# Two piece buffers in the accumulator for the first part, and another order of the projection pieces, in a two-layer hybrid mixer kernel

## The reference, cut to what matters

```python
def hybrid_layer(x, ...):
    h = rmsnorm(x, pre_norm)
    proj = einsum('bld,de->ble', h, w_in)          # columns of all three mixers and their gates
    o_a = rmsnorm(gated_deltanet(silu(conv(q,k,v)), ...)) * silu(gz)   # 4 heads of 128, chunk recurrence
    o_b = rmsnorm(ssd(silu(conv(x,B,C)), ...) * silu(sz))              # 2 groups of 8 heads
    o_c = rmsnorm(retention(rotary(q), rotary(k), v)) * silu(rg)       # 4 heads of 128
    out = einsum('ble,ed->bld', concat(o_a, o_b, o_c), w_out)
    return x + rmsnorm(out, post_norm)
```

## Time and profile before

| | us |
|---|---|
| median of 3 runs | 2120.73 (2119.14 to 2121.55) |
| the profiled execution | 2119.12 |
| its span, first to last instruction | 2117.3 |
| PE (matmul) busy | 2044.3 (97%) |
| PE weight loads busy | 1880.9 (89%) |
| DVE busy | 1416.7 (67%) |
| ACT busy | 878.2 (41%) |
| POOL busy | 482.3 (23%) |

### The profile page before, as it was taken

How to read it: one execution, slowest core, us unless ns; L and a number is a source line. 1 busy time by engine, 2 the same in 40 slices (tenths; PEclk the granted TensorE clock), 3 DMA queues, 4 the chain that set the end, 5 groups by cost and what they waited for, 6 DMA issues and landing times. The chain is left out here.

```text
span 2117.3 us, 38295 instructions
## 1 busy us (share of the span) xinstructions
PE 2044.3 (97%) x14628; PEld 1880.9 (89%) x14628; DVE 1416.7 (67%) x3428; ACT 878.2 (41%) x1771; POOL 482.3 (23%) x432
## 2 busy tenths in 40 slices
PE   7989999999999999999999999999999999999997
PEld 6768889999889998899888888889989899989997
DVE  5788866745578787623668887875466878575334
ACT  5544367423433236511444433754324433563011
POOL 3433343432000012100333333423300001120001
PEclk9989999999999999999999999999999999999999
DMA  6754546668544365454575554857656354573434
GB/s 244 247 179 152 204 173 210 239 212 305 189 170 161 138 207 189 163 166 146 185 262 198 199 194 154 299 191 252 239 206 214 133 170 139 178 270 130 159 106 184
DMA packets 98198, 410.59 MB, mean 194 GB/s; under 512 B 11169, under 2 KB 12257, under 8 KB 84193
## 3 DMA queue, kind: packets, MB, share of 16 engines
q1 hardware_dynamic: 97440, 407.73, 55.1%
q10 hardware_dynamic: 576, 0.41, 0.1%
HBM read 256.93 MB, written 151.16 MB: 193 GB/s over the span
## 5 line engine op out<-in xcount | busy, mean ns | idle before, releaser
L1327 PE MATMUL ps<-w_hi,hT_hi 128*128 128x256 f32 x1792 | 524.3, 293 | 6.7 <-POOL w_low L2389 5.0
L1327 PE MATMUL ps<-w_hi,hT_lo 128*128 128x256 f32 x1792 | 503.4, 281 | 0.0
L1327 PE MATMUL ps<-w_low,hT_hi 128*128 128x256 f32 x1792 | 501.9, 280 | 0.0
L2389 POOL TENSOR_TENSOR w_low<-w_loaded,w_hi 128x512 fp32r<-128x512 f32 x208 | 283.5, 1381 | 429.0 <-ACT w_hi L2103 429.0
L1327 PEld LDWEIGHTS ps<-w_hi,hT_hi 128*128 128x128 f32 x1792 | 337.7, 188 | 13.7 <-POOL w_low L2389 6.3
L1327 PEld LDWEIGHTS ps<-w_low,hT_hi 128*128 128x128 f32 x1792 | 338.1, 189 | 4.4 <-issue 3.8
L1327 PEld LDWEIGHTS ps<-w_hi,hT_lo 128*128 128x128 f32 x1792 | 339.5, 189 | 0.0
L1327 PE MATMUL ps<-hT_hi,w_hi 128*128 128x512 f32 x768 | 319.5, 416 | 6.3 <-POOL w_low L2389 6.2
L1327 PE MATMUL ps<-hT_lo,w_hi 128*128 128x512 f32 x768 | 304.0, 396 | 0.0
L1327 PE MATMUL ps<-hT_hi,w_low 128*128 128x512 f32 x768 | 303.4, 395 | 0.0
L1327 PE MATMUL ps<-wo_parts,mixT_hi 128*128 128x256 f32 x960 | 270.0, 281 | 0.0
(11 more groups left out here) (215 smaller groups left out, 3792.6 us busy)
## 6 DMA issues: line engine op xcount, KB each, us to landing
w_loaded<-in_w_in SPq DMA_DIRECT2D x104, 512.0 KB, 5.0
w_split<-w_hi SPq DMA_DIRECT2D x52, 1024.0 KB, 8.2
w_split<-w_low SPq DMA_DIRECT2D x52, 1024.0 KB, 10.2
w_hi<-w_split SPq DMA_DIRECT2D x104, 512.0 KB, 6.3
w_low<-w_split SPq DMA_DIRECT2D x104, 512.0 KB, 7.1
wo_loaded<-in_w_out SPq DMA_DIRECT2D x32, 512.0 KB, 4.2
wk<-cum_rows SPq DMA_DIRECT2D x32, 512.0 KB, 5.0
wo_split<-wo_parts SPq DMA_DIRECT2D x32, 512.0 KB, 8.5
```

The lines of the kernel that those rows point to most:

```text
L1327: return nc.tensor.matmul(o, a, b, start=start, stop=stop)
L2389: tt(w_lo[at], wr[at], w_hi[at], ALU.subtract)\
```

## The change

It does four things. It swaps pieces in `PIECES`, so that gate pieces stand between the deltanet heads' pieces (the same 26 pieces, in all four parts). In part 0 it gives deltanet heads 2 and 3 buffers of their own in `acc` (`SPARE` = 2, `slot_at`), and so moves on who has to be through before a buffer is used again (`slot_owner`). It writes the rule for split and kept pieces as functions with an exception list `AGAIN`, which is empty. And it changes numbers of the planner. No arithmetic of the kernel changes. The diff, cut: left out are the other places where `slot[:, n % SLOTS, ...]` becomes `slot_at(n)[:, ...]`, and the planner's and engines' uses of `is_split` and `is_kept`, which replace `p % 2 == 0`.

```diff
-PIECES = ([("gz", 0), ("gdn", 0), ("gdn", 1), ("gz", 1), ("bc", 0), ("gdn", 2), ("gdn", 3), ("bc", 1),
-           ("gdn", 4), ("sz", 0, 0), ("gdn", 5), ("sx", 0, 0), ("sx", 0, 1), ("sz", 0, 1), ("sx", 1, 0), ("sz", 1, 0),
+PIECES = ([("gz", 0), ("gdn", 0), ("gdn", 1), ("gz", 1), ("bc", 0), ("gdn", 2), ("bc", 1), ("gdn", 3),
+           ("sz", 0, 0), ("gdn", 4), ("sz", 0, 1), ("gdn", 5), ("sz", 1, 0), ("sx", 0, 0), ("sx", 0, 1), ("sx", 1, 0),
            ("sx", 1, 1), ("sz", 1, 1)]
           + [("ret", i) for i in range(N_RET)])
+AGAIN = range(0)
 SLOTS = 2
+SPARE = 2
...
             elif part == "sum":
-                mark("n", dve(900, *after))
+                mark("n", dve(1200, *after))
...
             elif part == "column":
-                mark("n", dve(len(cols) * 2 * (150 + 2 * BASE), *after))
+                mark("n", dve(len(cols) * 2 * (220 + 2 * BASE), *after))
...
-OUT_WAIT = 2500
+OUT_WAIT = 4000
-KEEP = 8
+KEEP = 2
-HOLD = 0
+HOLD = 250
-SLICE, LINE, TURN, UNIT, TABLE, MB, LANDING = 705, 224, 109, 24 * 119, 1283, 3500, 2300
+SLICE, LINE, TURN, UNIT, TABLE, MB, LANDING = 705, 224, 109, 24 * 119, 1283, 3300, 2000
...
+def is_split(n):
+    p, i = divmod(n, len(PIECES))
+    return p % 2 == 0 or i in AGAIN
+def is_kept(n):
+    p, i = divmod(n, len(PIECES))
+    return p % 2 == 0 and i not in AGAIN
...
+def slot_owner(n):
+    if n is None or n < SLOTS + SPARE:
+        return None
+    return n - SLOTS - SPARE if n < 2 * SLOTS + SPARE else n - SLOTS
...
 def frees(p, i, half):
     need = []
     n = slot_of(p, i, half)
-    if n is not None and n >= SLOTS:
-        need.append(slot_reader(n - SLOTS))
+    if slot_owner(n) is not None:
+        need.append(slot_reader(slot_owner(n)))
...
+        def slot_at(n):
+            if SLOTS <= n < SLOTS + SPARE:
+                return acc[:, 2 * (n - SLOTS):2 * (n - SLOTS) + 2, :].rearrange("p t d -> p (t d)")
+            return slot[:, n % SLOTS, :]
...
-                        sp.wait_ge(w_kept[n % W_RING], kept_done(n - W_RING))
+                        if kept_done(n - W_RING):
+                            sp.wait_ge(w_kept[n % W_RING], kept_done(n - W_RING))
```

More of the change, by code:

```diff
@@ L215, in front_steps @@
                     j, odd = divmod(Q * half + q - SPLIT_FROM, 2)
-                    if 0 <= j < 4 and not odd and (p + (i == len(PIECES) - 1)) % 2 == 0 and (p, i) != (PARTS - 1, len(PIECES) - 1):
+                    if 0 <= j < 4 and not odd and len(PIECES) * p + i + 1 < PARTS * len(PIECES) and is_split(len(PIECES) * p + i + 1):
                         add(("split", *((p, i + 1) if i + 1 < len(PIECES) else (p + 1, 0)), j))
@@ L264, in load_piece @@
         for half in range(2):
-            at["w_in", n, half] = dma(MB if n // len(PIECES) % 2 else MB // 2, *after)
+            at["w_in", n, half] = dma(MB // 2 if is_split(n) else MB, *after)
     def loaded_after():
@@ L278, in needs @@
             kk = q if wide else 2 * q % KD
-            out = [("w_in", n, kk // 4) if p % 2 else ("w_lo", n, kk // 2)] if half == 0 else []
+            out = [("w_lo", n, kk // 2) if is_split(n) else ("w_in", n, kk // 4)] if half == 0 else []
             if q == 0:
@@ L418, in play @@
                 load_piece(n + W_RING, ("n", ))
-            elif p % 2 == 0:
+            elif is_kept(n):
                 dma(2 * MB, ("w_lo", n, 3))
@@ L805, in unit_split_no @@
     return u - GROUPS * UNITS * ((u // (GROUPS * UNITS) + 1) // 2)
+def is_split(n):
[4 more added lines that the diff above has]
+    return p % 2 == 0 and i not in AGAIN
 def split_no(n):
-    return n - len(PIECES) * ((n // len(PIECES) + 1) // 2)
+    return sum(is_split(m) for m in range(n))
 def loads_done(n):
-    return sum(32 if m // len(PIECES) % 2 else 16 for m in range(n % W_RING, n + 1, W_RING))
+    return sum(16 if is_split(m) else 32 for m in range(n % W_RING, n + 1, W_RING))
 def kept_done(n):
-    return sum(32 for m in range(n % W_RING, n + 1, W_RING) if m // len(PIECES) % 2 == 0)
+    return sum(32 for m in range(n % W_RING, n + 1, W_RING) if is_kept(m))
 def slot_of(p, i, half):
@@ L1086, in mtile @@
                 n = slot_of(p, i, half)
-                return 24 * p + NTH[m], m, slot[:, n % SLOTS, (m % 3) * HALF:(m % 3 + 1) * HALF]
+                return 24 * p + NTH[m], m, slot_at(n)[:, (m % 3) * HALF:(m % 3 + 1) * HALF]
             if kind == "bc":
@@ L1093, in mtile @@
                 n = slot_of(p, i, half)
-                return 24 * p + NTH[16 + 4 * g + j], 16 + 4 * g + j, slot[:, n % SLOTS, j * HALF:(j + 1) * HALF]
+                return 24 * p + NTH[16 + 4 * g + j], 16 + 4 * g + j, slot_at(n)[:, j * HALF:(j + 1) * HALF]
             return None
@@ L1120, in hybrid_kernel @@
             loads.append((where[release] if n >= W_RING else -5 if n == 0 else -2, n, ("in", p, i)))
-            if p % 2 == 0:
+            if is_kept(n):
                 loads.append((where["proj", p, i, 0, Q - 1], n, ("keep", p, i)))
@@ L1156, in slot_wait @@
         def slot_wait(eng, n):
-            if n is None or n < SLOTS:
+            if slot_owner(n) is None:
                 return
-            r = slot_reader(n - SLOTS)
+            r = slot_reader(slot_owner(n))
             if r[0] == "gdn_open":
@@ L1383, in _ @@
                         if half == 0 and kk % 2 == 0 and (wide or v == 0):
-                            if p % 2 == 0:
+                            if is_split(n):
                                 pe.wait_ge(S["w_lo_ready"], 4 * split_no(n) + kk // 2 + 1)
@@ L1441, in _ @@
                         for c in range(NT):
-                            i = turn(b[:, c * P:(c + 1) * P], slot[:, n % SLOTS, j * HALF + c * P:j * HALF + (c + 1) * P])
+                            i = turn(b[:, c * P:(c + 1) * P], slot_at(n)[:, j * HALF + c * P:j * HALF + (c + 1) * P])
                         close(i, tag)
@@ L1445, in _ @@
                     h = s[2]
-                    own = slot[:, (10 * p + h) % SLOTS, :]
+                    own = slot_at(10 * p + h)[:, :]
                     b = opened(s)
@@ L1562, in _ @@
                         for j in range(4):
-                            i = turn(b[:, j * P:(j + 1) * P], slot[:, n % SLOTS, j * HALF + c * P:j * HALF + (c + 1) * P])
+                            i = turn(b[:, j * P:(j + 1) * P], slot_at(n)[:, j * HALF + c * P:j * HALF + (c + 1) * P])
                         close(i, tag)
@@ L1609, in _ @@
                     oo = ("ret_oo", p, h)
-                    vv = slot[:, (10 * p + 6 + h) % SLOTS, 1024:1536].rearrange("p (t n) -> p t n", t=NT)
+                    vv = slot_at(10 * p + 6 + h)[:, 1024:1536].rearrange("p (t n) -> p t n", t=NT)
                     if c == 0:
@@ L1734, in _ @@
                             dve.wait_ge(S["ret_sum"], m)
-                        own = slot[:, (10 * p + 6 + h) % SLOTS, half * 512:half * 512 + 512]
+                        own = slot_at(10 * p + 6 + h)[:, half * 512:half * 512 + 512]
                         b = bank(tag).rearrange("p (t q e n) -> p t q e n", t=2, q=2, e=2)
-                        ns = slot[:, (10 * p + 6 + h) % SLOTS, 0:1024].rearrange("p (t q e n) -> p t q e n", t=NT, q=2, e=2)
+                        ns = slot_at(10 * p + 6 + h)[:, 0:1024].rearrange("p (t q e n) -> p t q e n", t=NT, q=2, e=2)
                         r0 = own.rearrange("p (t q e n) -> p t q e n", t=2, q=2, e=2)
```

8 lines of the change are left out of this document (4 added, 4 removed).

## The result

The changed kernel takes 2142.39 us in the median of 4 runs (2136.62 to 2144.84), the kernel before 2119.93 beside it: a ratio of 1.0099, 95% interval 1.0087 to 1.0111. It is 22.5 us slower. I had forecast 2105.

The account below looks back on a forecast made before the run. PE was taken as the bound nearly everywhere, with gains only from its idle time and half clock. 8 + 4 + 3 = 15 us off 2119.1 gave 2104, forecast as a 2105 median (chance 0.52, range 2097 to 2114).

Parts of the forecast that it names:

- Step 4: Planner's new numbers, outside part 0: PE steps placed where they can run; -3 us, bounds -8 and +10.
- Step 1: Part 0: the wait at gdn 4 goes, the gap moves to sz 1 0; gain 8 us, bounds -3 and +14.
- t: Part 0: time of deltanet head 1's mix_turn, 220.22 us before; taken as 217, between 211 and 228.
- the late one: Part 0, late end for t: head 0 among projections, 4 chunks by 1.5 us, 226, or 228 with half clock.
- the early one: Part 0, early side for t: once PE is dry, DVE has only the chain; not much before 211.
- Step 2: Part 0, from t to head 3's mix_turn: most of 6.4 us idle filled; gain 4 us, bounds 0 and +6.
- My first rival: Part 0: the gap moves, nothing is gained; t is 225, splitting takes the later gain; 2119 us, chance 0.17.
- Step 3: Parts 1 to 3, same order without spare buffers: costed at nothing, 2.7 us a part without an output unit left.
- The tail: PE full from 1600 to 2100 us, so KEEP and HOLD move nothing but the order; 0, within 1 us.
- step 5: Edits with no effect: empty AGAIN, unchanged DMA queues, acc buffers read out before the first output unit; no wait added.
- The rival "slower": Part 0: sz 1 0 waits for head 1's late turn, PE dry; from t = 229; 2130 us, chance 0.13.
- What would show it wrong: Signs: second turn before 207; fourth turn after 300 with DVE as full; part 2's idle 13.3 us growing over 3 us.

Follow-up runs that it names:

- e5: Changed kernel with the planner's old numbers, so new order and spare buffers only: 2129.1 us, ratio 1.0045 to the kernel before.
- e1: Kernel before with the new order of pieces alone, no spare buffers, old planner numbers: 2132.0 us, ratio 1.0054.
- e16: New order alone, but the first group's gates moved back behind the fifth and sixth delta pieces; no spare buffers, old numbers: 2120.4 us, ratio 0.9998.
- e21: Changed kernel with the first group's gates behind the fifth and sixth delta pieces; spare buffers and new numbers kept: 2147.5 us, ratio 1.0131.
- e13: Kernel before with one move alone, the second group's gate from the 16th to the 13th piece: 2124.2 us, ratio 1.0018.
- e2_spare: Kernel before with the two spare buffers alone, old order, old planner numbers: 2128.4 us, ratio 1.0040.
- e20: New order with the first group's gates behind the fifth and sixth delta pieces, plus two spare buffers, old numbers: 2139.9 us, ratio 1.0094 to the kernel before.
- e15: Kernel before with the new order alone and the x pieces' convolutions 32 columns wide instead of 512: 2130.7 us, ratio 1.0050.
- e14: Kernel before with the two spare buffers alone and the x pieces' convolutions 32 columns wide instead of 512: 2122.2 us, ratio 1.0017.

## Why the prediction was wrong

**What bounds the kernel** was read rightly: PE nearly everywhere, and gains only from its idle time and clock.

**Where the 37 us went.** I forecast 15 us less and got 22.5 more. Steps 1 to 3 were to bring 12 us, and order and buffers together cost 9 (e5). Step 4 was to bring 3, and the numbers cost 13 on top.

**Step 1 failed by its size, 1 us instead of 8.** The wait came as told: the gap of 144 to 161 us goes, the next one is that of `sz 1 0` for head 1's turn, with a clock of 0.77 from 200 to 225 us. But t was 223.55, not 217. The fourteenth load was issued at 202.4 and not 8 but 22.6 us ahead of the earlier trace rows's 224.99, and the front then stood until `sz 1 0` at 224.3, where the old kernel was at 225. Both reasons that I gave for t miss. By the late one, four chunks of head 0 among projections cost 6 us; they took 17.9 us, before 17.7. By the early one, DVE would have only the chain once PE is dry, and t would come before 220.22; it came later in e1, e5 and e16 as well (221.6, 224.6 and 223.5), and of the kernels with buffers only e21 was earlier, by 1.3 us (218.9). In the changed kernel the loss of time is in head 1, before PE is dry. Its second chunk is on time, 185.49 before and 184.85 now, and its fourth comes at 203.82 instead of 198.22:

```profile
184.85 0.61 PE L1355 MATMUL ps<-st_g,wk 128*128 128x128 f32 x4
...
203.82 0.71 PE L1355 MATMUL ps<-st_g,wk 128*128 128x128 f32 x4 [1.46 <-DVE st_g L1913]
```

Between the two stand 21 slices of projection and two convolution operations, before 15 and none. e1, the order alone, has 20 slices there and takes 20.0 us; e16 has 15 and takes 12.7, as before. But e16's turn is at 223.5 all the same, so what sets t is not shown. What the runs do show is that t hardly moves ahead when the front does, and that the front then stops for it. By 200 us the changed kernel has lost 31.9 us and the one before 42.8, and from 200 to 250 us they lose 17.6 and 4.3.

**Step 2 came in at first and was lost again.** The idle time from 225 to 300 us fell from 6.4 to 1.7 us, as forecast, and PE waited 6.0 us for `w_low` instead of 8.1, so denser splitting cost nothing. But head 3's turn came at 302.48, 2.6 us after the earlier trace rows's 299.85. At 300 us the changed kernel was 3.7 us ahead in loss. The eighteenth piece began at 306.4 instead of 320.5, and yet `ret 0` at 362.6 instead of 364.1, each just behind the turn of the first state-space group (360.9 and 362.3). I had no term for the stages after head 3's turn, and there 3.2 of the 3.7 us went. My first rival, "the gap moves and nothing is gained", gives part 0's result, 0.6 us of gain at its end, though not by its reason, splitting.

**Step 3 is the largest wrong term of the order.** The order in parts 1 to 3 was costed at nothing, with 2.7 us a part if the units run out. It is nothing in part 1, but +15.2 us in part 2 with the order alone. I asked only for the wait that the gate ahead of the x pieces meets, head 1's turn, and that one was covered. I didn't ask what the gates behind which the delta pieces now stand do to head 3, whose turn the eighteenth piece needs. In step 2 I had worked out that very ceiling for part 0 ("just no new gap"), and didn't repeat it for part 2, where the trace before already had the turn at 1333.6 and the last free piece's end at 1337.3. A gate piece of 11.25 us more ahead of `gdn 5` doesn't fit into those 3.7 us; its last slice came 26 us later and the turn 23. The earlier trace rows was misread as well: at 1278 us PE was in the last slices of `sz 0 1`, and `sx 0 0`, before which I put that wait of 3.05 us, had started at 1230.9. Forced output units, the danger that I did name, are worth 3.5 us (e13).

**Step 4 had the wrong sign.** -3 with bounds of -8 and +10; measured +13 on order and buffers, +28 alone. That a new cost is nearer to its row is no argument for a better plan: the plan as a whole was laid well, and OUT_WAIT alone, the transfers' pair and the inverse's pair each lose 14 us or more. The tail was right: from the first retention turn of part 3 to the end are 167.2 us before and 166.9 after. But PE from 1600 on isn't as full, idle for 6.5 us instead of 1.9, for the gap at 1788 to 1813. Nothing spoke against step 5.

**The rival "slower"** had the right kind, PE dry while waiting for a turn, and the wrong place (head 1 instead of head 3) and price: 2130. Its condition, t of 229 us or more, wasn't met, and it had no term for the numbers. The result lies above it.

**What would show it wrong** named part 2's idle time: 13.4 us before in the two windows of the earlier trace rows, 22.1 after. The clock adds to it. The other sign, the fourth turn later than 300 us with DVE as full, showed too (302.48). Of the two rules of the Trainium skill that I cited, the one in "TensorE: Matmul & The Clock Gate", section "HAM oscillation — how this bites in real kernels", on idle gaps, is borne out by the windows at 0.77 to 0.86 with gaps of 2 to 5 us in them. The other, from "Trainium Kernel Development and Optimization", "Best Practices", that weight loads' busy time shows the distance to the roof, gives the direction and half of the size: the room by it grew from 236.4 to 250.1 us (2143.0 - 1892.9), and the span by 25.7. The other 12.0 us are the loads' own time, which rose for the same 14628 loads, with a granted clock of 0.985 instead of 0.991.

## What to carry to other kernels

Work pulled into a wait is not yet a gain: here 10.9 us were won by 200 us and 13.3 lost in the next 50, since the turn at which the front stops next didn't come sooner. Ask what sets the next wait's end, and whether the filling itself gets between the steps of that chain. Before a piece without a chain is pulled ahead of pieces that start one, find for every stage the last turn that a later piece needs and how much free work lies before it; in part 2 that margin was 4 us. Constants of a planner are laid for each other; here every change of them that moved a step, truer or not, cost 14 us or more, so measure the plan anew after such an edit.

## What was not expected of the hardware

A gap has two prices, as the earlier trace rows already had it. Where PE idles among short chain steps its clock falls to 0.76 to 0.80 over 50 us (e2_spare, e20), and the matmuls that are there take longer: four of 128 columns 1.22 us at 207.45 in e2_spare, where 0.60 is shown at the full clock. And the convolutions' width mattered little: 32 columns instead of 512 for the 96 operations of the x pieces took 47 us off DVE's busy time in e15 (1417.0 to 1370.0), and 1.4 us off the median, within the noise; in e14 it was 51 us of DVE (1422.0 to 1370.9) and 6.2 us of the median. Nor is one such operation, 512 columns wide, always as long: of the 288 in the kernel before, the 197 during which POOL ran nothing took 0.75 us on average, and the 37 during which POOL was busy for at least 80% of the time 1.15 us, as far as POOL's records can be trusted.
